# Per-token norm roots as columns: DMA copies out of one partition in place of one-column matmuls and a second root

## What is computed

```python
def rmsnorm(x, g):
    xf = x.astype(jnp.float32)
    y = xf * lax.rsqrt(jnp.mean(xf * xf, axis=-1, keepdims=True) + RMS_EPS)
    return (y * g.astype(jnp.float32)).astype(x.dtype)

for l in range(DEPTH):                     # first block, DEPTH = 2
    h = rmsnorm(x, norm1[l])
    proj = h @ w_in[l]
    qa, ka, va, qb, kb, vb, gate_pre = jnp.split(proj, splits, axis=-1)
    ...

h = rmsnorm_2(x, norm_mix_g_2[layer])      # second block, odd layer
z = h @ w_in
q_m, k_m, v_m, o_m, gates, c_q, c_kv, k_r = jnp.split(z, ODD_SPLIT, axis=-1)
```

## Time and profile before

| | us |
|---|---|
| median of 3 runs | 2802.95 (2801.0 to 2803.54) |
| the profiled execution, a run of its own | 2793.8 |
| its span, first to last instruction | 2791.6 |
| TensorE busy | 2741.2 (98% of the span) |
| VectorE busy | 1532.4 (55%) |
| ScalarE busy | 1110.5 (40%) |
| GpSimd busy | 42.8 (2%) |
| mean granted TensorE clock | 0.995 of full speed |

### The profile page before, as it was taken

One profiled execution on the slowest core, in us unless ns is written; L12 is line 12 of the kernel. 1 busy time (PEld: TensorE's weight loads), 2 busy tenths in 40 slices (PEclk: granted clock), 3 DMA queues, 4 the chain that ended last, 5 costly groups with the idle time before them and its releaser, 6 DMA issues.

```text
span 2791.6 us, 33679 instructions
## 1 busy us (share of the span) xinstructions
PE 2741.2 (98%) x12745; PEld 2240.1 (80%) x12745; DVE 1532.4 (55%) x2107; ACT 1110.5 (40%) x1521; POOL 42.8 (2%) x36
## 2 busy tenths in 40 slices
PE   9999999999999999999999999999999999999998
PEld 7887788887888778888878878888878668788886
DVE  4376755455535675554667654434563556644344
ACT  3146544334313654432352443322442654533223
POOL 3000000000200000000000000000000000000000
PEclk9999999999999999999999999999999999999999
DMA  5221233332332123333243423333242114232322
GB/s 161 90 61 54 83 93 99 94 100 83 104 97 72 50 69 106 90 94 102 79 121 91 121 76 91 94 102 100 80 106 72 36 48 134 61 105 83 108 84 87
DMA packets 463902, 249.89 MB, mean 90 GB/s; under 512 B 21094, under 2 KB 459327, under 8 KB 463679
## 3 DMA queue, kind: packets, MB, share of 16 engines
q1 hardware_dynamic: 463807, 248.57, 31.1%
HBM read 246.44 MB, written 2.10 MB: 89 GB/s over the span
## 4 chain that ended last, share of the span: by engine, by line
PE 89%; DVE 6%; ACT 3%; issue 1%; DMA 1%; DVEq 0%; ACTq 0%; SPq 0%
PE M L711 26%; PE M L713 26%; PE M L712 26%; DVE w_lo L2134 1%; PE M L804 1%; PE M L806 1%; PE M L805 1%; PE A L901 1%; PE A L876 1%; PE A L711 1%; PE A L945 1%; PE A L712 1%; PE A L713 1%; PE A L890 0%; ACT w_hi L1514 0%
## 5 line engine op out<-in xcount | busy, mean ns | idle before, releaser
L711 PE MATMUL M<-h_hi,w_hi 128*128 128x512 f32 x2184 | 860.8, 394 | 1.0 <-issue 1.0
L713 PE MATMUL M<-h_hi,w_lo 128*128 128x512 f32 x2184 | 851.6, 390 | 0.0
L712 PE MATMUL M<-h_lo,w_hi 128*128 128x512 f32 x2184 | 851.4, 390 | 0.0
L1514 ACT ACTIVATE w_hi<-stage 128x1024 fp32r<-128x1024 f32 (+3 forms) x504 | 495.6, 1026 | 725.5 <-PE M L713 661.0
L2134 DVE TENSOR_TENSOR w_lo<-stage,w_hi 128x1024 fp32r<-128x1024 f32 (+3 forms) x504 | 584.7, 1198 | 148.4 <-ACT w_hi L1514 147.7
L711 PEld LDWEIGHTS M<-h_hi,w_hi 128*128 128x128 f32 x2184 | 410.6, 188 | 92.1 <-issue 5.7
L713 PEld LDWEIGHTS M<-h_hi,w_lo 128*128 128x128 f32 x2184 | 410.5, 188 | 86.6
L712 PEld LDWEIGHTS M<-h_lo,w_hi 128*128 128x128 f32 x2184 | 410.7, 188 | 86.2 <-issue 2.6
L711 PE MATMUL M<-hid_hi,w_hi 128*128 128x512 f32 x704 | 275.2, 391 | 7.0 <-DVE hid_lo L2272 7.0
L713 PE MATMUL M<-hid_hi,w_lo 128*128 128x512 f32 x704 | 274.0, 389 | 0.0
L712 PE MATMUL M<-hid_lo,w_hi 128*128 128x512 f32 x704 | 274.0, 389 | 0.0
(11 more groups left out here) (491 smaller groups left out, 3230.6 us busy)
## 6 DMA issues: line engine op xcount, KB each, us to landing
stage<-in_w_up SPq DMA_DIRECT2D x88, 512.0 KB, 4.5
stage<-in_ffn_w_gate_up SPq DMA_DIRECT2D x88, 512.0 KB, 4.7
stage<-in_w_in SPq DMA_DIRECT2D x80, 512.0 KB, 4.5
stage<-in_w_down SPq DMA_DIRECT2D x32, 384.0 KB, 3.7
stage<-in_ffn_w_down SPq DMA_DIRECT2D x32, 384.0 KB, 3.8
stage<-in_od_w_in SPq DMA_DIRECT2D x21, 512.0 KB, 4.0
stage<-in_w_down SPq DMA_DIRECT2D x32, 320.0 KB, 3.5
stage<-in_ffn_w_down SPq DMA_DIRECT2D x32, 320.0 KB, 3.5
```

What stands on the lines that cost most here:

```text
L711: pe.matmul(bank, a_hi, b_hi, start=(n == 0), stop=False)
L712: pe.matmul(bank, a_hi, b_lo, start=False, stop=False)
L713: last = pe.matmul(bank, a_lo, b_hi, start=False, stop=(n == k - 1))
L1514: act.activation(w_hi[:, s, part * HALF:part * HALF + n], stage[:, part, 0:n], ACT.Copy)\
```

## The change

The columns are no longer computed. SyncE waits until ScalarE has the row (`rstd_done`) and then copies it out of partition 0 by DMA: for each 128 tokens in natural order one DMA of 128 single floats, one to a partition, and for the residues one DMA of 128 pieces of four floats. In the first layer that is one DMA, in the second five, in the odd layer four. They are issued behind the load of chunk 4 of `qk0` and of `qk1`, and behind the load of chunk 0 of `od_in`. VectorE waits for `col_landed` in place of `col_done`. The one-column matmuls, the second root, the copy at L1796 and their waits go. Four vector transposes (L1072), the natural columns of the first layer and the final norm's columns stay as they are.

```diff
-        def columns_before(n):
+        def columns_through(n):
 
-            return sum(j < n for j in WITH_COLUMNS)
+            return sum((16, 80, 64)[i] for i, j in enumerate(WITH_COLUMNS) if j <= n)
...
+            def turn_row(n):
+
+                sp.wait_ge(rstd_done, n + 1)
+                for t in range(TT if n else 0):
+                    sp.dma_start(rstd_col[:, t:t + 1], rstd[0:1, t * P:(t + 1) * P].unsqueeze(2),
+                                 allow_slow_non_contiguous=True).then_inc(col_landed, 16)
+                if n < FINAL:
+                    sp.dma_start(rstd_col[:, TT:2 * TT], rstd[0:1, :].rearrange("o (p r) -> o p r", r=DIL[1]),
+                                 allow_slow_non_contiguous=True).then_inc(col_landed, 16)
...
                     if l or n >= 2:
                         load_tiles(c0 + n, tiles, m)
+                    if n == 4:
+                        turn_row(2 * l)
...
                 load_tiles(c0 + n, tiles, 2 * n)
+                if n == 0:
+                    turn_row(MIX[1])
...
                 pe.wait_ge(square_added, additions(n + 1))
-                if n in WITH_COLUMNS:
-                    for t in range(tokens // P):
-                        pe.matmul(A[1][:, t:t + 1], square_sum[:, t * P:(t + 1) * P], ones[:, 0:1], start=True, stop=True)
-                    if n < FINAL:
-                        for r in range(TT):
-                            pe.matmul(A[1][:, TT + r:TT + r + 1], by_residue(square_sum[:, :], 1)[:, r, :], ones[:, 0:1],
-                                      start=True, stop=True)
                 pe.matmul(A[0][:, 0:tokens], ones, square_sum[:, 0:tokens], start=True, stop=True)\
...
-                pe.wait_ge(rstd_done, 1)
                 pe.wait_ge(inputs_landed, 16 * INPUTS)
-                for r in range(TT):
-                    last = pe.matmul(A[1][:, r:r + 1], by_residue(rstd[0:1, :], 1)[:, r, :], ones[0:1, 0:1], start=True, stop=True)
-                last.then_inc(turned, 1)
...
-            pe.wait_ge(col_done, columns_before(MIX[1]) + 1)
...
-            def norm_columns(n, dst, count):
-
-                act.activation(dst[:, 0:count], A[1][:, 0:count], ACT.Ln, bias=eps[:, 0:1], scale=1.0 / D).then_inc(col_root, 1)
-                act.wait_ge(col_root, columns_before(n) + 1)
-                act.activation(dst[:, 0:count], dst[:, 0:count], ACT.Exp, scale=-0.5).then_inc(col_done, 1)
...
-                    act.wait_ge(turned, KT + 2)
-                    act.activation(rstd_col[:, TT:2 * TT], A[1][:, 0:TT], ACT.Copy).then_inc(col_done, 1)
-                    act.sem_inc(col_root, 1)
...
                     norm_rows(2 * l)
-                    norm_columns(2 * l, rstd_col, 2 * TT)
...
             norm_rows(MIX[1])
-            norm_columns(MIX[1], rstd_col, TT)
...
-                        dve.wait_ge(turned, KT + 3)
+                        dve.wait_ge(turned, KT + 2)
...
-                dve.wait_ge(col_done, columns_before(2 * l) + 1)
+                dve.wait_ge(col_landed, columns_through(2 * l))
...
-            dve.wait_ge(col_done, columns_before(MIX[1]) + 1)
+            dve.wait_ge(col_landed, columns_through(MIX[1]))
```

More of the change, by code:

```diff
@@ L383, in block_program @@
         perm_done = sem("perm_done")
-        branch_done, value_done, col_root, col_done = (
-            sem("branch_done"), sem("value_done"), sem("col_root"), sem("col_done"))
+        branch_done, value_done, col_landed = sem("branch_done"), sem("value_done"), sem("col_landed")
         final_square, final_added, final_root, final_mean, final_mix, x_final = (
```

## The result

| | before | changed |
|---|---|---|
| median | 2802.11 us, 6 runs (2799.11 to 2803.54) | 2787.53 us, 6 runs (2782.99 to 2791.29) |
| profiled execution, span | 2793.8, 2791.6 us | 2783.0, 2780.8 us |
| mean granted clock of it | 0.995 | 0.997 |

The ratio is 0.9948, 95% interval 0.9935 to 0.9961. The changed kernel is 14.6 us faster by the medians, where 7.4 was forecast; 2787.5 lies under the range. So the sign was right and the size was half of what happened.

The account below looks back on a forecast made before the run. TensorE's own queue was taken to set the time nearly everywhere; 5.7 us of matmuls plus 1.7 of clock made 7.4 off the median 2802.95, so 2795.6 us, with a range of 2791.5 to 2800.5.

Parts of the forecast that it names:

- The matmuls leave the queue: TensorE's queue loses 2.0 us in the first layer, 2.8 in the second, 0.9 in the odd: 5.7 us.
- The clock, one fall of 1.7 us: The fall of TensorE's clock right behind the first layer's place goes with the one-column matmuls: 1.7 us, between 0 and 5.1.
- The terms are stretches of TensorE's queue that every run has, I take the same off the median.: The 7.4 us summed for the profiled execution also come off the three runs' median, 2802.95, giving 2795.6 us.
- ScalarE's second root and VectorE's wait are hidden: Sparing ScalarE two activations of about 0.25 us twice, and VectorE a 0.62 us wait in the odd layer, gains nothing.
- The ten copies cost nothing: Ten DMAs on SyncE's queue, 3.6 us for five, fit the room of 18 and 14.5 us: no cost.
- The rival in which the copies block the loads: On SyncE's queue, copies run one after another at 6.5 us each and delay weight loads: 2821.6 us, chance 0.04.
- The estimate of 38 us: Time per DMA copy if the Trainium skill's 19× factor applied to a small load's 2.0 us; kernel far slower.
- The clock does not pay: Rival: the clock fall comes anyway, moves elsewhere or is absent in the median run; only 5.7 us, 2797.3, chance 0.32.
- the time is absorbed: Rival: a wait takes over behind one of the three places, leaving about 3.4 us, or 2799.6; chance 0.12.

Follow-up runs that it names:

- the wide kernels: Two variants of the changed kernel with unread 128x512 products taking the one-column matmuls' time, one also with an unread second root; mean 2793.0 us.
- e0_before: The kernel before, unchanged, run and profiled once more: ratio 0.9997 to the kernel before, median 2799.6 us, profiled execution 2801.3 us.
- e8_wide_root: The changed kernel with unread 128x512 products at the three places and an unread second root on ScalarE: ratio 0.9980 to the kernel before, median 2792.5 us.
- e9_after_root: The changed kernel with an unread second root put back on ScalarE: ratio 0.9963 to the kernel before, median 2787.5 us.
- e10_narrow2: The changed kernel with norm 2's one-column matmuls alone put back, unread, without a second root: ratio 0.9984 to the kernel before, median 2793.3 us.

## Why the prediction was wrong

- **The matmuls leave the queue, 5.7 us, all on the path.** Right: the three stretches came out at 0.51, 0.69 and 0.68 us, which is 5.7 off, and the wide kernels give 6.0 with an uncertainty of 0.8.
- **The clock, one fall of 1.7 us, taken between 0 and 5.1.** The mechanism was right and the size too small: 3.0 us in the mean. The profiled execution had one fall behind three places, and the prediction took this one picture for the usual one. A fall behind the first place came in two of six profiles, one behind norm 2 in four of eight, so neither the fall of the earlier trace rows nor its clock of 1.00 in the second layer is the rule. The falls right behind the places are fewer than two in an execution; the rest of the 3.0 us is in falls that stand elsewhere.
- **"The terms are stretches of TensorE's queue that every run has, I take the same off the median."** This step failed most. The profiled execution was 9 us under the median of its own runs. I had set this difference aside as something that the trace cannot show, and gave it no term, not even a bound. e0_before shows what most of it can be: the collision, up to 8.0 us in a part of the executions, 3.6 to 3.9 in the mean, and the change takes it away. (The three runs behind that median have no trace of their own.) The view that could have warned is the earlier trace rows with GpSimd's and VectorE's rows beside it: the sixteen copies start there, and four of them took twice as long as the others.
- **ScalarE's second root and VectorE's wait are hidden.** Right as far as tested: e8_wide_root and e9_after_root put the root back, for -0.5 and +0.8 us, both without one-column matmuls beside it.
- **The ten copies cost nothing.** Right in the result. An issue took 0.6 us, not 0.4; landing 2.6 to 4.6 us against 2.0; the queue was held for 3.2 us (the 3.6 counted a landing too), and four times as many still fit. The rival in which the copies block the loads needed 4.4 us of queue for each. The estimate of 38 us, from the factor of 19 of the Trainium skill, DMA: Bandwidth & Descriptors, Rules for kernel authors, is not borne out by these copies of 128 single floats: they landed after 3.4 us.
- **The other rivals.** "The clock does not pay" and "the time is absorbed" gave 2797.3 and 2799.6, and neither happened; the fall behind the first place went with the matmuls, the four transposes alone did not bring it, and no new wait came up.
- **The range** reached down to two falls of the clock. It had nothing for the difference between the profile and the median. Of the 14.6 us between the first medians 12.8 are left over all executions; the rest is the scatter of the first six.

## What to carry to other kernels

When the profiled execution lies some us off the median of its runs, there can be a term in the others that this trace does not show: take a second profile, or put that difference into the range, before adding up what a change saves. Count one-column matmuls at their queue time and about half as much again for the clock: here 5.7 and 3.0 us for 32 records. Where GpSimd runs a row of copies while VectorE makes something that TensorE needs next, hold GpSimd's row back behind VectorE's work if its results are wanted later; here that alone was worth 3.9 us to the kernel before.

## What the chip did that I had not expected

- GpSimd's copies of 1.1 us each, back to back, kept one operation of VectorE that takes 1.2 us from finishing for 11.6 us (e10_narrow2); in e0_before nine copies began in that time without a pause; in the execution in front, of the same program, VectorE got in after one.
- The clock goes down right behind 2.8 us of one-column matmuls, in four of eight profiles, though TensorE shows busy all the time, and each fall takes 1.7 us or a multiple of it: 1.7, 3.4 and 5.1 were all the sizes seen ahead of the last 12 us in 16 profiles.
- A fall does not stay where its cause is: kernels without the one-column matmuls show falls too, at 224, 1646 and 2236 us among others. Ahead of the last 12 us they add up to 7.6 us in the mean of the seven profiles without one-column matmuls and to 12.9 in that of the nine with some. One that stands ahead of a wait is mostly made up: the wait for `stay_hi` is 2.1 us without a fall ahead of it and 0.5 with one.
- The ten copies out of one partition into 128 partitions, eight of them of 128 single floats, landed in 2.6 to 4.6 us in the changed kernel's profile, and stood 0.6 us apart on the queue.
